# Two transformer blocks on one core: the first block's query projection cut into nine full tiles, and four moves around it

## The reference, cut to what matters

```python
proj = hn @ w_in_a[j]                       # 1024 -> 384 + 256 + 32 + 256 + 1024
c_q, c_kv, k_r, q_m, gate = split_cols(proj, [Q_LORA, KV_LORA, MLA_ROPE, MEM_WIDTH, MIX_WIDTH])
q = (rms_norm(c_q, q_norm) @ w_q_up).reshape(B, S, MLA_HEADS, MLA_QK)      # 12 heads of 96 columns
q_nope, q_rope = q[..., :MLA_NOPE], rope(q[..., MLA_NOPE:], pos)           # 64 plain, 32 rotary
kv = (rms_norm(c_kv, kv_norm) @ w_kv_up).reshape(B, S, MLA_HEADS, MLA_NOPE + MLA_V)
out = causal_block_attention(qf, kf, v, MLA_QK ** -0.5)
y = jnp.concatenate([main, mem_out.reshape(B, S, MEM_WIDTH)], axis=-1) * jax.nn.silu(gate)
h = h + rms_norm(y @ w_out[i], norm_post[i])
hn = rms_norm(h, norm_pre[i + 1]); proj = hn @ w_in_b[j]                   # the next layer
mod = jnp.matmul(silu(c), ada_w[layer]) + ada_b[layer]                     # second block, computed on the side
```

## Time and profile before

| | us |
|---|---|
| median of 3 runs (lowest, highest) | 2020.9 (2020.48, 2022.31) |
| the profiled execution's own time | 2023.0 |
| its span, first to last instruction | 2021.3 |
| PE busy in it | 1959.0 (97%) |
| mean granted clock of TensorE | 0.991 |

### The profile page before, as it was taken

One profiled execution on the slowest core, in us unless ns is written; L12 is line 12 of the kernel. 1 busy time (PEld: TensorE's weight loads), 2 busy tenths in 40 slices (PEclk: granted clock), 3 DMA queues, 4 the chain that ended last, 5 costly groups with the idle time before them and its releaser, 6 DMA issues.

```text
span 2021.3 us, 23916 instructions
## 1 busy us (share of the span) xinstructions
PE 1959.0 (97%) x9938; PEld 1543.3 (76%) x9938; DVE 1031.0 (51%) x1529; ACT 766.9 (38%) x1171; POOL 784.7 (39%) x347
## 2 busy tenths in 40 slices
PE   7999999999999999999999999999999999999998
PEld 5875666788767698977788888877977877788776
DVE  5325577556776748733566646664911343311323
ACT  5333664422364432165433223324376333312331
POOL 2232553334464452213244334344433433444342
PEclk9999999999999999999999999999999999999999
DMA  7223103356402152121334543453440222233221
GB/s 237 85 58 79 57 1 115 105 169 188 146 1 84 63 179 92 63 63 42 105 125 143 165 150 125 130 157 95 138 131 24 72 84 95 68 105 119 76 74 60
DMA packets 203404, 205.71 MB, mean 102 GB/s; under 512 B 12023, under 2 KB 199675, under 8 KB 203296
## 3 DMA queue, kind: packets, MB, share of 16 engines
q1 hardware_dynamic: 200809, 200.31, 31.2%
q0 software_dynamic: 1472, 3.72, 0.7%
q10 hardware_dynamic: 1015, 0.16, 0.1%
HBM read 201.20 MB, written 2.11 MB: 101 GB/s over the span
## 4 chain that ended last, share of the span: by engine, by line
PE 76%; DVE 8%; POOL 7%; ACT 6%; issue 2%; DMA 1%; ACTq 0%; DVEq 0%; SPq 0%
PE bank L540 43%; PE bank L1125 16%; POOL wl L2341 6%; ACT wh L1336 3%; PE bank L781 2%; PE bank L481 2%; DVE conv L2225 1%; PE bank L805 1%; PE bank L948 1%; DVE conv L2227 1%; PE bank L830 1%; DVE conv L2223 1%; PE bank L1183 1%; PE bank L1193 1%; DVE acc L1777 1%
## 5 line engine op out<-in xcount | busy, mean ns | idle before, releaser
L2341 POOL TENSOR_TENSOR wl<-ring,wh 128x2048 fp32r<-128x2048 f32 (+4 forms) x146 | 620.0, 4247 | 962.0 <-ACT wh L1336 960.3
L1336 ACT ACTIVATE wh<-ring 128x2048 fp32r<-128x2048 f32 (+4 forms) x146 | 256.0, 1754 | 298.1 <-PE bank L1125 129.9
L1777 DVE SCALAR_TENSOR_TENSOR acc<-ring,cs,acc 128x256 f32<-128x256 f32 x336 | 281.3, 837 | 12.0
L540 PE MATMUL bank<-xfh,wh 128*128 128x512 f32 x704 | 277.1, 394 | 7.0 <-POOL wl L2341 7.0
L540 PE MATMUL bank<-xfh,wl 128*128 128x512 f32 x704 | 274.3, 390 | 0.0
L540 PE MATMUL bank<-xfl,wh 128*128 128x512 f32 x704 | 274.0, 389 | 0.0
L540 PEld LDWEIGHTS bank<-xfh,wh 128*128 128x128 f32 x704 | 132.1, 188 | 42.0 <-POOL wl L2341 11.6
L540 PEld LDWEIGHTS bank<-xfh,wl 128*128 128x128 f32 x704 | 132.1, 188 | 27.9
L540 PEld LDWEIGHTS bank<-xfl,wh 128*128 128x128 f32 x704 | 132.2, 188 | 26.5
L1125 PE MATMUL bank<-hsph,wh 128*128 128x512 f32 x352 | 138.8, 394 | 2.3 <-POOL wl L2341 2.3
L1125 PE MATMUL bank<-hsph,wl 128*128 128x512 f32 x352 | 137.7, 391 | 0.0
(11 more groups left out here) (407 smaller groups left out, 4117.1 us busy)
## 6 DMA issues: line engine op xcount, KB each, us to landing
ring<-in_ada_w SPq DMA_DIRECT2D x48, 1024.0 KB, 5.3
ring<-in_ffn_w_in SPq DMA_DIRECT2D x44, 1024.0 KB, 5.1
ring<-in_w_in_b SPq DMA_DIRECT2D x14, 1024.0 KB, 5.3
ring<-in_even_w_in SPq DMA_DIRECT2D x14, 1024.0 KB, 5.1
ring<-in_ffn_w_out SPq DMA_DIRECT2D x16, 768.0 KB, 4.4
ring<-in_odd_w_in SPq DMA_DIRECT2D x12, 1024.0 KB, 6.0
ring<-in_ffn_w_out SPq DMA_DIRECT2D x16, 640.0 KB, 4.1
ring<-in_w_out SPq DMA_DIRECT2D x8, 1024.0 KB, 5.3
```

Of the source, the lines that this page charges most:

```text
L540: mm = eng.matmul(o, l_, r_, start=(first and i == 0), stop=(last and i == 2))
L1336: eng.activation(wh[:, m % SPLIT, h:w], ring[:, n % RING, h:w], ACT.Copy).then_inc(wh_ready, 1)
L1777: ins = eng.scalar_tensor_tensor(out=s, in0=w[:, k, :], scalar=cs[:, k:k + 1], in1=s, op0=ALU.mult, op1=ALU.add)
L2341: eng.tensor_tensor(wl[:, m % SPLIT, h:w], ring[:, n % RING, h:w], wh[:, m % SPLIT, h:w].bitcast(F32), ALU.subtract).then_inc(wl_ready, 1)
```

## The change

- `w_q_up` is read in three chunks: all rotary columns (12 heads of 32, three tiles), then the plain columns of eight heads (four tiles of two heads) and of four heads (two tiles). The first chunk needs three DMAs with runs of 32 elements, the others three each with runs of 64.
- The three rotary tiles go to a buffer `qr`; the matrix that turns is 128 x 128 (four heads at once). Three rotations stand behind the first three plain tiles. DVE makes two products of 128 x 512 for each and four sums of 32 x 512 into `qf`. ACT empties a plain tile with two copies of 64 x 512.
- Constants grow from 673 to 769 columns; positions and angles now fill 128 partitions.
- At the start `warm(2)` becomes `warm(3)`, and behind the spread of the norm `warm(2)` becomes `warm(7)`.
- `SHARED` is empty for the first layer: DVE adds all eight tiles there. POOL makes the low part of `in_b.f` without an addition ahead of it.
- ACT makes the high part of v0 ahead of the root of the next norm, not behind it.
- One of the four `ada_steps` comes ahead of `log_sigmoid`.

```diff
-SHARED = (1, 3, 5)
+SHARED = ((), (1, 3, 5))
...
-C_ID, C_ONE, C_NINCL, C_NONE, C_CAUSAL, C_ROT, C_FREQ = 0, 128, 256, 384, 512, 640, 672
-C_COLS = 673
+C_ID, C_ONE, C_NINCL, C_NONE, C_CAUSAL, C_ROT, C_FREQ = 0, 128, 256, 384, 512, 640, 768
+C_COLS = 769
...
-    q = a["w_q_up_a"][0].rearrange("(t p) n -> p t n", p=P)
-    add([("q_up", q[:, :, n * 576:(n + 1) * 576], 3, 576) for n in range(2)])
+    q = a["w_q_up_a"][0].rearrange("(t p) (h n) -> p t h n", p=P, n=NOPE + ROPE)
+    add([("q_rope", q[:, :, :, NOPE:], 3, HEADS * ROPE), ("q_nope", q[:, :, 0:8, 0:NOPE], 3, 8 * NOPE),
+         ("q_nope", q[:, :, 8:HEADS, 0:NOPE], 3, (HEADS - 8) * NOPE)])
...
-            warm(2, n=S // 2)
+            warm(3, n=S // 2)
             norm_spread((mem_normed, KT), 2)
-            warm(2, n=S // 2)
+            warm(7, n=S // 2)
...
+            m, ws = chunk("q_rope")
+            for j in range(3):
+                features(("qr", j), "act", ws, slice(j * P, (j + 1) * P), cqs, 3, "cq")
+            chunk_done(m)
             h = 0
-            for _ in range(2):
-                m, ws = chunk("q_up")
-                for j in range(6):
-                    features(("q", h), "act", ws, slice(96 * j, 96 * (j + 1)), cqs, 3, "cq")
-                    if h >= 1:
-                        rotate = h - 1
-                        b = bank(("qrot", rotate), "dve")
-                        wait_emptied(pe, ("q", rotate))
-                        done(eng.matmul(b[ropes, :], rot, qf[ropes, rotate, :], start=True, stop=True))
-                    h += 1
+            for pairs in (4, 2):
+                m, ws = chunk("q_nope")
+                for j in range(pairs):
+                    features(("q", h), "act", ws, slice(j * P, (j + 1) * P), cqs, 3, "cq")
+                    h += 2
+                    if h <= 6:
+                        b = bank(("qrot", h // 2 - 1), "dve")
+                        wait_emptied(pe, ("qr", h // 2 - 1))
+                        done(eng.matmul(b[:, :], rot4, qr[:, h // 2 - 1, :], start=True, stop=True))
                 chunk_done(m)
-            b = bank(("qrot", HEADS - 1), "dve")
...
-            eng.dma_start(pos_i[ropes, :], a["positions"][0].partition_broadcast(ROPE)).then_inc(loaded_p, 16)
+            eng.dma_start(pos_i[:, :], a["positions"][0].partition_broadcast(P)).then_inc(loaded_p, 16)
...
-            for h in range(HEADS):
-                empty(("q", h), qf[0:96, h, :], part=(slice(0, 96), slice(0, S)))
+            for j in range(3):
+                empty(("qr", j), qr[:, j, :])
+            for name, dst in (("q", qf), ("k", kf)):
+                for h in range(0, HEADS, 2):
+                    split_weights(tile_chunk[index[(name, h)]] + 2)
+                    b = take(act, (name, h), "act")
+                    eng.activation(dst[0:NOPE, h, :], b[0:NOPE, :], ACT.Copy)
+                    eng.activation(dst[0:NOPE, h + 1, :], b[NOPE:P, :], ACT.Copy).then_inc(emptied["act"], 1)
...
                     square(x[:, t, :])
+                if l == 0:
+                    split_weights(tile_chunk[index[("in_b.gate", 0)]] + 3)
                 root()
...
+            for j in range(3):
+                if j == 1:
                     dve.wait_ge(kr_ready, 1)
-                if h >= 2:
-                    dve.wait_ge(rope_done, h - 1)
-                rotate(("qrot", h), qf[ropes, h, :], h % 2).then_inc(rope_done, 1)
+                if j == 2:
+                    dve.wait_ge(rope_done, 4)
+                turned_parts(("qrot", j), qr[:, j, :], j % 2, slice(0, P))
+                for i in range(P // ROPE):
+                    part = slice(i * ROPE, (i + 1) * ROPE)
+                    eng.tensor_tensor(qf[ropes, 4 * j + i, :], rt[part, j % 2, :], rt[part, 2 + j % 2, :], ALU.add
+                                      ).then_inc(rope_done, 1)
...
             empty_scaled(("f",), frow[0:HEADS, 0, :], slice(0, HEADS))
+            ada_steps(1)
...
-            ada_steps(4)
+            ada_steps(3)
...
             attention(0)
-            low_weights(tile_chunk[index[("out_a", KT - 1)]] + 2)
-            residual(0)
             low_weights(tile_chunk[index[("out_a", KT - 1)]] + 3)
```

More of the change, by code:

```diff
@@ L100, in constants @@
     half = ROPE // 2
-    for r in range(half):
-        c[NOPE + r + half, C_ROT + r] = -1.0
-        c[NOPE + r, C_ROT + r + half] = 1.0
+    for base in range(0, P, ROPE):
+        for r in range(base, base + half):
+            c[r + half, C_ROT + r] = -1.0
+            c[r, C_ROT + r + half] = 1.0
     freq = np.float32(10000.0) ** (-np.arange(half, dtype=np.float32) / np.float32(half))
-    c[NOPE:NOPE + ROPE, C_FREQ] = np.concatenate([freq, freq])
+    c[:, C_FREQ] = np.tile(freq, 2 * P // ROPE)
     m = np.zeros((P, len(HG_LEVELS) + 1, P), np.float32)
@@ L304, in two_block_kernel @@
         ropes = slice(NOPE, NOPE + ROPE)
-        rot = consts[ropes, C_ROT:C_ROT + ROPE]
-        freq = consts[ropes, C_FREQ:C_FREQ + 1]
+        rot4 = consts[:, C_ROT:C_ROT + P]
+        rot = rot4[ropes, ropes]
+        freq = consts[:, C_FREQ:C_FREQ + 1]
         sq_sum = at("sq_sum", 110, S)
@@ L322, in two_block_kernel @@
         cqs, ckvs, kr = pair("cqs", 80, 86, 3, S), pair("ckvs", 92, 96, 2, S), at("kr", 100, S)
-        rt = at("rt", 48, 4, S)
+        rt, qr = at("rt", 48, 4, S), at("qr", 106, HEADS * ROPE // P, S)
         qf, kf = at("qf", 0, HEADS, S), at("kf", 24, HEADS, S)
@@ L1302, in _ @@
                     for t in range(kt):
-                        eng.dma_start(dst[:, t, :].rearrange("p (h n) -> p h n", h=HEADS), src[:, t]
+                        eng.dma_start(dst[:, t, :].rearrange("p (h n) -> p h n", h=src.shape[2]), src[:, t]
                                       ).then_inc(landed[n % RING], 16)
@@ L1439, in _ @@
                     act.wait_ge(angle_ready, 1)
-                    eng.activation(sin[ropes, :], sin[ropes, :], ACT.Sin).then_inc(sin_ready, 1)
-                    eng.activation(cos[ropes, :], cos[ropes, :], ACT.Sin).then_inc(sin_ready, 1)
+                    eng.activation(sin[:, :], sin[:, :], ACT.Sin).then_inc(sin_ready, 1)
+                    eng.activation(cos[:, :], cos[:, :], ACT.Sin).then_inc(sin_ready, 1)
                     load_roots()
@@ L1458, in _ @@
                 empty(("in_a.gate", t), gate[:, t, :], ACT.Silu)
-            for h in range(HEADS):
-                empty(("q", h), qf[0:96, h, :], part=(slice(0, 96), slice(0, S)))
-            for h in range(0, HEADS, 2):
-                split_weights(tile_chunk[index[("k", h)]] + 2)
-                b = take(act, ("k", h), "act")
-                eng.activation(kf[0:NOPE, h, :], b[0:NOPE, :], ACT.Copy)
-                eng.activation(kf[0:NOPE, h + 1, :], b[NOPE:P, :], ACT.Copy).then_inc(emptied["act"], 1)
+            for j in range(3):
[6 more added lines that the diff above has]
+                    eng.activation(dst[0:NOPE, h + 1, :], b[NOPE:P, :], ACT.Copy).then_inc(emptied["act"], 1)
             act.wait_ge(rope_done, HEADS)
@@ L1511, in out_first @@
                 for t in range(KT):
-                    if t in SHARED:
-                        act.wait_ge(x_shared, l * len(SHARED) + SHARED.index(t) + 1)
+                    if t in SHARED[l]:
+                        act.wait_ge(x_shared, SHARED[l].index(t) + 1)
                     else:
-                        act.wait_ge(x_added, l * (KT - len(SHARED)) + t + 1 - sum(u < t for u in SHARED))
+                        act.wait_ge(x_added, l * KT + t + 1 - sum(u < t for u in SHARED[l]))
                     if l == 0:
@@ L1899, in _ @@
             dve.wait_ge(loaded_p, 48)
-            pr = posf[ropes, :]
-            tr = turn[ropes, :]
-            sr, cr = sin[ropes, :], cos[ropes, :]
-            chain.link(eng.tensor_copy(pr, pos_i[ropes, :]))
+            pr = posf[:, :]
+            tr = turn[:, :]
+            sr, cr = sin[:, :], cos[:, :]
+            chain.link(eng.tensor_copy(pr, pos_i[:, :]))
             chain.link(eng.tensor_scalar(pr, pr, freq, None, ALU.mult))
@@ L2008, in out_first @@
                                                  ).then_inc(xl_ready, 1)
-                    if 1 <= t <= KT and t - 1 not in SHARED:
+                    if 1 <= t <= KT and t - 1 not in SHARED[l]:
                         dve.wait_ge(post_scaled, l * KT + t)
@@ L2365, in residual @@
             def residual(l):
-                for t in SHARED:
+                for t in SHARED[l]:
                     pool.wait_ge(post_scaled, l * KT + t + 1)
```

14 lines of the change are left out of this document (5 added, 9 removed).

## The result

The changed kernel takes **1994.65 us** (median of 4 runs, 1992.4 to 1995.13), the kernel before 2020.69 beside it: ratio 0.9867, 95% interval 0.985 to 0.9884, which is 26 us faster. The profiled execution took 1992.4 (span 1990.7); that of before had taken 2023.0, so the profiled pair differs by 30.6, more than the medians do. Why is part of what follows.

What follows compares the result with a forecast made beforehand. PE (TensorE), holding 76% of the chain, was taken as the bound. Queries −12.0, start −1.6, between the layers −2.5 and v2 −5.85 made −22.0: 2023.0 to 2001.0 profiled, median 1999 us, range 1994 to 2005.

Steps and rivals of the forecast that it cites:

- the gap of 2.5 us before the keys: Queries to keys: two tiles left, 4.1 us, do not cover making the keys' parts; PE newly waits 2.55 us.
- no wait before v0 or v2: Between the layers: PE's waits of 1.50 us before v0 and 3.35 before v2 vanish; v2 still late, chance 0.15.
- The loads: Query chunks: 4608 runs of 128 B land in 7.4 us; late chunks halving the queries' gain, 2005 to 2011, chance 0.04.
- The rival of short runs: Query and key loads: short runs cost more, eating the gain at 6.4 ns each; kernel slower, chance 0.03.
- the likeliest case: Whole kernel: the forecast itself, 1997 to 2001 us, chance 0.53.
- the 0.4 charged to constants and positions: Start: larger constants and 192 KB more of positions ahead of the second memory chunk make it 0.4 us late.
- The rotation at 1.18: Queries: each 128 x 128 rotation with the start after it costs 1.18 us, as the old one did.
- The clock before the keys: Keys: after PE's new gap the clock is low, charged 1.7 us; no such penalty and larger effects, chance 0.08.
- The clock at the start, −2.0: Memory's values: seven warm matmuls hold the clock, saving 2.0 us; low here and longer before keys, chance 0.15.
- Between the layers, −8.35: First layer's additions to v2: −2.5 us up to v0 and −5.85 for v2.
- The terms without any clock: Whole kernel: keys begin 13.7 us earlier, start 0.4 later, hand-over to v0 −2.5, v2's wait of 3.35 gone.
- The terms of clock: Whole kernel: full clock at the memory's values −2.0 us, low clock before the keys +1.7, full clock at v2.

Runs made afterwards that it cites:

- step_behind: The changed kernel with all four ada steps behind the logarithm of the forget gates, as before the change: 2000.41 us, ratio 0.991 to the kernel before.
- rotation_96_by_96: The kernel before with the rotation matmul contracting over 96 partitions and giving 96 result columns: 2016.01 us, ratio 0.9984 to the kernel before.
- queries_alone: The kernel before with only the new queries (nine tiles, three rotations, three chunks, wider positions): 2003.15 us, ratio 0.9924.
- after_again: The changed kernel once more, unaltered: 1993.43 us, ratio 0.9874 to the kernel before.
- fill_undone: The changed kernel with two unread matmuls instead of seven behind the spread of the memory's norm: 1997.13 us, ratio 0.9891 to the kernel before.
- after_third: The changed kernel a further time, unaltered, as standard for variants sent with it: 1992.87 us, ratio 0.9877 to the kernel before.
- root_first: The changed kernel with the high part of v0 behind the root of the next norm again: 1995.67 us, ratio 0.9882 to the kernel before.
- additions_shared: The changed kernel with POOL adding tiles 1, 3 and 5 in the first layer again: 1994.94 us, ratio 0.9879 to the kernel before.
- start_alone: The kernel before with only warm(3) and warm(7) at the start: 2017.96 us, ratio 0.9992.
- handover_alone: The kernel before with only first-layer additions all on DVE, v0's high part ahead of the root, one ada step ahead of log_sigmoid: 2009.02 us, ratio 0.9948.
- two_pairs_first: The changed kernel with the plain columns of four heads ahead of those of eight, loads too: 1988.25 us, ratio 0.9847 to the kernel before.
- gap_filled: The changed kernel with three unread matmuls in PE's gap before the keys: 1991.46 us, ratio 0.9864 to the kernel before.

## Why the prediction was right and where it was wrong

**Right, by its own steps.** The waits and the feeding came as worked out: 27 matmuls fewer; the gap of 2.5 us before the keys (2.55 forecast), ended by POOL's `wl`; a part of x every 2.15 us; no wait before v0 or v2, v2 in time by 1.1 us (1.4 forecast) with a step stretched by POOL. The loads were no matter. The rival of short runs is answered by the DMA issues between 118 and 160 us (count, KB, us to landing):

```profile
ring<-in_w_q_up_a SPq DMA_DIRECT2D x2, 192.0 KB, 3.9
ring<-in_w_q_up_a SPq DMA_DIRECT2D x3, 128.0 KB, 2.6
```

192 KB in runs of 128 B are 1536 runs in 3.9 us, 2.5 ns each at most. That is more than the 1.6 that the prediction took from the keys' row, and far from the 6.4 at which it would have decided.

**Wrong: the sum of −22.0 was about 4 us too small,** and the time fell at the lower edge of the range, outside the 1997 to 2001 of the likeliest case. No wait and no path of the changed stages was wrong. What failed is what the steps were priced at. The distances between starts of PE in the 15 profiles show where (us; in brackets the number of profiles; "rest" is all behind v2; kernels that vary a stage's own edit are left out of its row):

| stage | without its edit | with it | forecast | found |
|---|---|---|---|---|
| memory's values to queries | 134.7 to 135.6 (6) | 131.6 to 131.8 (8), 135.9 (*step_behind*) | −2.0 | −3.1 in the mean |
| queries | 38.4 (4) | 23.7 (9) | −13.7 | −14.7 |
| keys to scores | 17.5 (4) | 17.5 (4), 18.8 to 19.1 (4) | +1.7 | +0.7 in the mean |
| scores to first part of x | 139.6 to 139.7 (4) | 139.1 to 139.2 (changed kernel, 3) | 0 | −0.5 |
| first part of x to v0 | 26.2 (5) | 23.5 (8) | −2.5 | −2.7 |
| v0 to the end of v2 | 41.9 to 42.1 (5) | 35.8 to 36.0 (9) | −5.85 | −6.1 |
| rest | 1595 to 1601 | the same | 0 | 0 |

With nothing for the 0.4 charged to constants and positions, the last column makes −26.4, and the medians gave 26.0. Term by term:

- *The rotation at 1.18: the first step that failed.* The prediction held that the stationary's width doesn't enter, and that nine matmuls of 96 columns in 2.25 us cost what those of the gate do. Its own rows have 0.227 for one of these, 2.05 for nine. It took the old price for the new rotation, with 0.97 as the lower end for the matmul; it measured 0.87 with the start behind it. Three of them make 0.9 us. The old price held a surcharge that goes with the narrow result, as *rotation_96_by_96* shows.
- *The clock before the keys, charged in full: the second.* The low clock came there in the profiles of 4 of the 8 kernels that have this gap (*queries_alone*, *after_again*, *fill_undone*, *step_behind*), and not in the changed kernel, *after_third*, *root_first* and *additions_shared*. Where it came the keys up to the scores took 18.8 to 19.1 us, otherwise 17.5. It is a cost of about 1.4 us half the time, so some 0.7 and not 1.7.
- *The clock at the start, −2.0: the third.* The fill took away a second stretch, near 104 us, that the prediction did not have in its sum: it was low there in all six profiles without the fill, and at full clock in eight of the nine with it. That is about 1.3 us more. Against this *start_alone*, which has only the fill, gained 1.6 by its median, and taking the fill out of the whole cost 3 to 4, so the size is not sharp.
- *Between the layers, −8.35.* The stages measure −2.7 to v0 and −6.0 up to the end of v2 in the profiled pair, which is nearly the forecast. In medians *handover_alone* gained 10.5; some 1 of the 2 us more is again clock in stretches that the prediction did not speak of. The 0.5 between the scores and the first part of x has no term in it. *queries_alone* is 0.3 shorter there and *handover_alone* 0.15; by what is not shown.

The terms without any clock were −13.7, +0.4, −2.5 and −3.35, together −19.2; at equal clock it measured −21.2 ± 0.9. Of these 2.0 the rotation is 0.9, and the rest is hardly more than the interval. The terms of clock were −2.0, +1.7 and −2.5, together −2.8; it measured −4.3. The clock terms failed because the low clock was read as something bound to the one gap in front of it, from one profile. That it is low after each gap over 2.8 us held in the rows of that profile; at the first part of x such a gap (2.88 or 2.89) was followed by it in 4 of 6 profiles, and one of 2.75 in 1 of 9. The stretch there, from which the 1.7 was taken, cost nothing in its own place: up to v0 it is 26.2 us in the kernel before, with the low clock, and in *start_alone* and *queries_alone*, without it.

**What the profile of before hid.** It was itself one draw. Ahead of its last microseconds it has seven low stretches, 34 us long together, more than any other profile, and its mean clock of 0.991 equals the lowest of the 53 timed executions of this kernel (0.991 to 0.995). It also had the memory tokens land at 8.62 us, where every other profile has 7.0 to 8.0. Behind v2, where nothing was changed, it is 2.5 us longer than the changed kernel's first profile, and it begins 1.0 later on the memory's values. That is most of why the profiled pair differs by 30.6 and the medians by 26.

**Left open.** Which execution gets a low stretch is not settled. PE is idle before the first part of x (at 352 us in the kernel before) in all 15 profiles, for 2.88 or 2.89 us in the six where POOL shares the additions and for 2.75 in the nine others; the clock was low around its end in four of the six and in one of the nine. Whether the tenth of a microsecond matters is not shown. In the changed kernel single stretches came at 646 and 1288 us in one execution, at 1287 in another, and at neither in a third. Nor is it settled why *two_pairs_first* and *gap_filled* lose those too: with one profile each that may be chance. The Trainium skill, page "TensorE: Matmul & The Clock Gate", section "What's actually happening", calls the point at which the clock rises in the first matmuls run-variable, since it depends on where in a free-running window they land. It says this of the rise; the counts here are of the fall, and no run here tests whether the same is behind them.

## What to carry to other kernels

Work out the feed of a multi-engine stage on the clock of the old trace, and ask of each chunk how much work of PE is left to cover the next one's parts: it gave the new gap within 0.1 us, and the cure as well, the small chunk of plain columns ahead of the large one. Before the price of an operation is carried over to another shape, compare its neighbours in the rows too: here 2.25 against 2.05 us for nine matmuls was the sign of the surcharge. Read the granted clock from more than one profile, or compare at equal clock, before a microsecond of it enters a sum: here it was worth as much as the smaller edits, and it moved by 9 us between executions of one kernel. Undo each edit on top of the whole too; taking the moved ada step out of the whole cost 7.5 us, where the trace of before had promised 5.85.

## What the runs showed of the hardware

- A narrow result between wider ones costs PE time: a full float32 matmul with a result of 32 columns (on partitions 64 to 95) between product tiles of 96 costs 1.17 us beyond the nine products, and 0.87 with a result of 96 columns between them, or 128 between tiles of 128. The rows contracted over (32 or 96) make no difference. Whether the width or the place of the result does it is not shown.
- POOL's parts hold up small operations of DVE too, hidden here: DVE's four sums of 32 x 512 took 2.83 us for the first two rotations and 9.17 for the third, which ran beside POOL's two low parts (172.18 to 179.95):

```profile
167.15 2.83 DVE L1957 TENSOR_TENSOR qf<-rt 32x512 f32<-32x512 f32 x4
...
171.33 9.17 DVE L1957 TENSOR_TENSOR qf<-rt 32x512 f32<-32x512 f32 x4
```

- An idle of 3.4 us of PE at the start was followed by the low clock in 6 of 6 profiles, one of 3.3 to 5.1 before v2 in 6 of 6, one of 2.88 before the first part of x in 4 of 6, one of 2.75 there in 1 of 9, one of 2.5 before the keys in 4 of 8, and one of 1.3 to 1.6 at the start in 0 of 9.
